# Loads of x in two halves around the first weights, the bias table as high and low parts, splits of x and of weights in turn

## The reference, cut to what matters

```python
def first_block(x, ...):
    h = rmsnorm(x, norm_mix[0])
    x = x + short_conv_mixer(h, conv_w_in[0], conv_w[0], conv_w_out[0])   # h @ w_in comes first
    ...
def differential_attention(q, k, v, lam, rel_bias):
    bucket = t5_bucket(k_pos[None, :] - q_pos[:, None])
    bias = rel_bias[bucket].astype(jnp.float32).transpose(2, 0, 1)         # 32 buckets, 4 heads
    s = jnp.einsum('bhcqd,bhcsd->bhcqs', qblk, kt).astype(jnp.float32) * scale + bias[None, :, None]
```

## Time and profile before

| | |
|---|---|
| median of three runs | 1386.07 us |
| fastest of them | 1385.76 us |
| profiled execution, its own time | 1391.24 us |
| its span, first to last instruction | 1389.4 us |
| PE busy | 1317.0 us, 95% |
| DVE busy | 1035.0 us, 74% |
| ACT busy | 855.5 us, 62% |
| first matmul of the weight stream | 19.62 us after the start of the span |

### The profile page before, as it was taken

How to read it: one execution, slowest core, us unless ns; L and a number is a source line. 1 busy time by engine, 2 the same in 40 slices (tenths; PEclk the granted TensorE clock), 3 DMA queues, 4 the chain that set the end, 5 groups by cost and what they waited for, 6 DMA issues and landing times.

```text
span 1389.4 us, 18772 instructions
## 1 busy us (share of the span) xinstructions
PE 1317.0 (95%) x6058; PEld 1073.3 (77%) x6058; DVE 1035.0 (74%) x1471; ACT 855.5 (62%) x1256; POOL 35.7 (3%) x48
## 2 busy tenths in 40 slices
PE   7999999998897999999999999999998885999998
PEld 5878888887576788888888888888876754888887
DVE  4576555567546999999999999999994846555554
ACT  4656444457344687878787878788774544544443
POOL 0000000001100000000000000000000301000000
PEclk9999999999798999999999999999999875999999
DMA  9545555554121897989898989998994400355440
GB/s 360 215 151 185 189 195 187 181 173 161 63 86 64 307 373 298 367 318 362 315 369 310 362 315 366 344 352 330 335 346 152 182 1 1 143 184 188 182 151 31
DMA packets 46121, 319.31 MB, mean 230 GB/s; under 512 B 5152, under 2 KB 6304, under 8 KB 7808
## 3 DMA queue, kind: packets, MB, share of 16 engines
q1 hardware_dynamic: 44288, 316.40, 61.0%
q10 hardware_dynamic: 1680, 2.10, 0.5%
q0 software_dynamic: 112, 0.26, 0.2%
HBM read 316.64 MB, written 2.10 MB: 229 GB/s over the span
## 4 chain that ended last, share of the span: by engine, by line
PE 85%; DVE 9%; ACT 2%; issue 2%; DMA 1%; DVEq 0%; POOL 0%; SPq 0%; ACTq 0%
PE bank L360 25%; PE bank L362 25%; PE bank L361 24%; PE bank L741 3%; DVE wl L1399 2%; PE bank L424 2%; DVE x L1906 2%; PE bank L847 1%; PE bank L396 1%; ACT wh L932 1%; DMA fixed<-fixed_dram 1%; PE bank L604 1%; PE bank L603 1%; PE bank L868 1%; DVE xtl L1419 1%
## 5 line engine op out<-in xcount | busy, mean ns | idle before, releaser
L1399 DVE TENSOR_TENSOR wl<-raw,wh 128x1024 fp32r<-128x1024 f32 x598 | 713.6, 1219 | 217.4 <-ACT wh L932 207.5
L932 ACT ACTIVATE wh<-raw 128x1024 fp32r<-128x1024 f32 x598 | 630.1, 1059 | 326.8 <-PE bank L362 319.6
L360 PE MATMUL bank<-wh,xth 128*128 128x512 f32 (+2 forms) x1170 | 467.1, 399 | 10.1 <-DVE wl L1399 4.7
L362 PE MATMUL bank<-wh,xtl 128*128 128x512 f32 (+2 forms) x1170 | 457.3, 391 | 0.0
L361 PE MATMUL bank<-wl,xth 128*128 128x512 f32 (+2 forms) x1170 | 457.0, 391 | 0.0
L360 PEld LDWEIGHTS bank<-wh,xth 128*128 128x128 f32 x1170 | 223.1, 191 | 56.4 <-issue 6.4
L362 PEld LDWEIGHTS bank<-wh,xtl 128*128 128x128 f32 x1170 | 222.6, 190 | 46.8
L361 PEld LDWEIGHTS bank<-wl,xth 128*128 128x128 f32 x1170 | 223.4, 191 | 42.5
L360 PE MATMUL bank<-wh,hth 128*128 128x512 f32 x456 | 178.5, 391 | 0.0
L362 PE MATMUL bank<-wh,htl 128*128 128x512 f32 x456 | 177.9, 390 | 0.0
L361 PE MATMUL bank<-wl,hth 128*128 128x512 f32 x456 | 177.4, 389 | 0.0
(11 more groups left out here) (288 smaller groups left out, 786.1 us busy)
## 6 DMA issues: line engine op xcount, KB each, us to landing
raw<-weights_dram SPq DMA_DIRECT2D x299, 1024.0 KB, 5.3
x<-x_dram SPq DMA_DIRECT2D x1, 1024.0 KB, 8.0
bias_scratch<-act ACTq DMA_DIRECT2D x1, 1024.0 KB, 15.8
wide<-bias_scratch ACTq DMA_DIRECT2D x8, 128.0 KB, 2.3
out_dram<-x SPq DMA_DIRECT2D x4, 256.0 KB, 2.1
fixed<-fixed_dram SPq DMA_DIRECT2D x1, 600.0 KB, 9.1
rows<-rows_dram POOLq DMA_DIRECT2D x1, 256.0 KB, 6.1
cols<-cols_dram SPq DMA_DIRECT2D x1, 73.0 KB, 8.8
```

The source lines that it names most:

```text
L360: mm(o, lh, wh[:, wi, sl], start=start, stop=False)
L362: return mm(o, ll, wh[:, wi, sl], start=False, stop=stop)
L932: A(wh[:, c % SPLIT, 0:n], raw[:, (c // 2) % RAW, (c % 2) * UNIT:(c % 2) * UNIT + n], ACT.Copy).then_inc(hi_done, 1)
L1399: V.tensor_tensor(wl[:, c % SPLIT, 0:n], raw[:, (c // 2) % RAW, (c % 2) * UNIT:(c % 2) * UNIT + n], f32(wh[:, c % SPLIT, 0:n]), ALU.subtra ...
```

## The change

- SP issues only the identity part of `fixed` early, then `cols`, the first 512 columns of x (half 0), weight panel 0, the other half of x, panel 1, the rest of `fixed`, and panels 2 to 5. Each half of x has its own semaphore.
- The spread bias table is split in a high and a low part (fp32r), and the selector is copied to fp32r. Each head is then two fp32r matmuls. Heads 0 and 1 are multiplied before the transposes of half 0, heads 2 and 3 between those of half 0 and of half 1. PE waits for the copies of heads 0 and 1 before unit 0, and for those of heads 2 and 3 before unit 4.
- ACT touches a small tile first, so that the function table is loaded there. ACT and DVE then alternate: two blocks of x, one weight unit, four times, and then units 4 and 5. DVE copies heads 2 and 3 after unit 1.
- The table goes to DRAM in four transfers, one for each head, from other tiles. ACT does not wait for them before the first layer; it waits before the read-back, and DVE waits before the first SwiGLU.
- Some semaphores are merged, with no change in the order of the work.

```diff
-            sp.dma_start(x[:, :, :], x_in.rearrange("(t p) d -> p t d", p=P)).then_inc(sem("x_in"), 16)
-            sp.dma_start(fixed[:, :], fixed_in).then_inc(sem("fixed_in"), 16)
+            sp.dma_start(fixed[:, 0:P], fixed_in[:, 0:P]).then_inc(sem("cols_in"), 16)
             sp.dma_start(cols[:, :], cols_in).then_inc(sem("cols_in"), 16)
-            for p in range(RAW):
+            halves = x_in.rearrange("(t p) d -> p t d", p=P)
+            sp.dma_start(x[:, :, 0:WIDE], halves[:, :, 0:WIDE]).then_inc(sem("x_in0"), 16)
+            sp.dma_start(raw[:, 0, :], weights[0]).then_inc(raw_full[0], 16)
+            sp.dma_start(x[:, :, WIDE:D], halves[:, :, WIDE:D]).then_inc(sem("x_in1"), 16)
+            sp.dma_start(raw[:, 1, :], weights[1]).then_inc(raw_full[1], 16)
+            sp.dma_start(fixed[:, P:NFIXED], fixed_in[:, P:NFIXED]).then_inc(sem("fixed_in"), 16)
+            for p in range(2, RAW):
                 sp.dma_start(raw[:, p, :], weights[p]).then_inc(raw_full[p], 16)
...
-            pe.wait_ge(sem("rel_in"), 32)
-            for h in range(NB2):
-                mm(bank[h][:, :], relw[:, h, :], onehot, start=True, stop=True).then_inc(sem("rel_T"), 1)
-            pe.wait_ge(sem("fixed_in"), 16)
-            for n in range(2):
-                turn_half("mix0", n, 4 + 2 * n)
-            pe.wait_ge(sem("rel_c"), NB2)
+            def rel_bias(h):
+                mm(bank[h][:, :], relh[:, h, :], picked, start=True, stop=False)
+                mm(bank[h][:, :], rell[:, h, :], picked, start=False, stop=True).then_inc(sem("rel_T"), 1)
+            rel_bias(0)
+            rel_bias(1)
+            pe.wait_ge(sem("cols_in"), 32)
+            turn_half("mix0", 0, 4)
+            rel_bias(2)
+            rel_bias(3)
+            turn_half("mix0", 1, 6)
...
             for j in range(6):
+                if j < 2:
+                    pe.wait_ge(sem("rel_c"), 2 * j + 2)
...
-            sc.wait_ge(sem("cols_in"), 16)
-            for n in range(2):
-                turned_hi("mix0", n, 4 + 2 * n)
-            for c in range(SPLIT):
+            sc.wait_ge(sem("half"), 1)
+            A(stat[:, 0:1], half[:, 0:1], ACT.Copy)
+            sc.wait_ge(sem("cols_in"), 32)
+            for c in range(4):
+                turned_hi_pair("mix0", 2 * c, 4 + c)
+                split_hi(c, 0)
+            for c in range(4, SPLIT):
                 split_hi(c, 0)
             for n in range(2):
                 squares("mix0", n)
-            sc.wait_ge(sem("rel_c"), NB2)
-            sc.dma_start(scratch[0:NB2 * P, :].rearrange("(h p) n -> p h n", p=P), act[:, 0, 0:NB2 * WIDE].rearrange("p (h n) -> p h n", h=NB2))\
-              .then_inc(sem("rel_st"), 16)
+            for h in range(NB2):
+                sc.wait_ge(sem("rel_c"), h + 1)
+                sc.dma_start(scratch[h * P:(h + 1) * P, :], rel_rows[h]).then_inc(sem("rel_st"), 16)
             sc.wait_ge(sem("ang"), 1)
             A(trig[:, :, :, :], trig[:, :, :, :], ACT.Sin).then_inc(sem("trig"), 1)
-            sc.wait_ge(sem("rel_st"), 16)
...
-            V.tensor_copy(relw[:, :, :], relb[:, :, None].to_broadcast((BUCKETS, NB2, P))).then_inc(sem("rel_w"), 1)
-            for h in range(NB2):
+            spread = relb[:, :, None].to_broadcast((BUCKETS, NB2, P))
+            mark(V.tensor_copy(picked, onehot.rearrange("p (a n) -> p a n", a=2)))
+            link(V.tensor_copy(relh, spread))
+            V.tensor_tensor(rell, spread, f32(relh), ALU.subtract).then_inc(sem("rel_w"), 1)
+            def rel_copy(h):
                 dv.wait_ge(sem("rel_T"), h + 1)
-                V.tensor_copy(act[:, 0, h * WIDE:(h + 1) * WIDE], bank[h][:, :]).then_inc(sem("rel_c"), 1)
-            dv.wait_ge(sem("cols_in"), 16)
-            turned_lo("mix0", range(0, 4), 4)
-            turned_lo("mix0", range(4, 8), 6)
-            for c in range(SPLIT):
+                V.tensor_copy(rel_rows[h], bank[h][:, :]).then_inc(sem("rel_c"), 1)
+            rel_copy(0)
+            rel_copy(1)
+            dv.wait_ge(sem("cols_in"), 32)
+            for c in range(4):
+                for k in (2 * c, 2 * c + 1):
+                    dv.wait_ge(sem("norm_hi"), 2 * c + 2)
+                    V.scalar_tensor_tensor(out=xtl[:, k, :], in0=bank[4 + c][:, (k % 2) * 256:(k % 2 + 1) * 256],
+                                           scalar=col("mix0", k), in1=f32(xth[:, k, :]), op0=ALU.mult, op1=ALU.subtract)\
+                     .then_inc(sem("norm_l"), 1)
                 split_lo(c, 0)
-
+                if c == 1:
+                    rel_copy(2)
+                    rel_copy(3)
+            for c in range(4, SPLIT):
+                split_lo(c, 0)
```

More of the change, by code:

```diff
@@ L177, in build @@
         onehot = ebuf[0:BUCKETS, 0, :]
-        relw = ebuf[0:BUCKETS, 1, :].rearrange("p (h n) -> p h n", h=NB2)
+        picked = hth[0:BUCKETS, 0:2, :]
+        relh, rell = (v[0:BUCKETS, 2:4, :].rearrange("p a (h n) -> p (a h) n", h=2) for v in (hth, htl))
+        rel_rows = (act[:, 0, 3072:3584], act[:, 1, 3072:3584], hbuf[:, 0, :], hbuf[:, 1, :])
         NORMS = ("mix0", "ffn0", "mix1", "ffn1", "attn2", "mlp2")
@@ L191, in x_ready @@
             if tag == "mix0":
-                eng.wait_ge(sem("x_in"), 16)
+                eng.wait_ge(sem(f"x_in{n}"), 16)
             elif tag == "attn2":
@@ L290, in _ @@
             g = nc.gpsimd
-            pool.dma_start(rows[:, :], rows_in.to_broadcast((P, NROWS))).then_inc(sem("rows_in"), 16)
+            pool.dma_start(rows[:, :], rows_in.to_broadcast((P, NROWS))).then_inc(sem("pos_in"), 16)
             pool.dma_start(posi[:, :], pos_in).then_inc(sem("pos_in"), 16)
@@ L314, in norm_rs @@
                 if tag in GATED:
[L315 to L318, removed]
+                    r.then_inc(sem("norm_gate"), 1)
+                    pool.wait_ge(sem("norm_gate"), 2 * GATED.index(tag) + 1)
+                    g.tensor_scalar(nrs[:, NT:2 * NT], nrs[:, 0:NT], 0.5, None, ALU.mult).then_inc(sem("norm_gate"), 1)
+                    pool.wait_ge(sem("norm_gate"), 2 * GATED.index(tag) + 2)
                     r = g.tensor_tensor(nrs[:, 2 * NT:3 * NT], nrs[:, 0:NT], nrs[:, NT:2 * NT], ALU.mult)
@@ L961, in turned_hi, with turned_hi_pair @@
                       scale=col(tag, 4 * n + k)).then_inc(sem("norm_hi"), 1)
+            def turned_hi_pair(tag, k0, b):
+                for k in (k0, k0 + 1):
+                    sc.wait_ge(sem("norm_T"), KD * nth(tag) + k0 + 2)
+                    A(xth[:, k, :], bank[b][:, (k % 2) * 256:(k % 2 + 1) * 256], ACT.Copy, scale=col(tag, k))\
+                        .then_inc(sem("norm_hi"), 1)
             def rs_ready(tag):
@@ L1300, in _ @@
                 squares("attn2", n)
+            sc.wait_ge(sem("rel_st"), 16 * NB2)
             for h in range(NB2):
@@ L1519, in _ @@
             dv.wait_ge(sem("rel_in"), 32)
-            V.tensor_copy(relw[:, :, :], relb[:, :, None].to_broadcast((BUCKETS, NB2, P))).then_inc(sem("rel_w"), 1)
-            for h in range(NB2):
-                dv.wait_ge(sem("rel_T"), h + 1)
-                V.tensor_copy(act[:, 0, h * WIDE:(h + 1) * WIDE], bank[h][:, :]).then_inc(sem("rel_c"), 1)
-            dv.wait_ge(sem("cols_in"), 16)
-            turned_lo("mix0", range(0, 4), 4)
-            turned_lo("mix0", range(4, 8), 6)
-            for c in range(SPLIT):
-                split_lo(c, 0)
-            dv.wait_ge(sem("pos_in"), 16)
+            spread = relb[:, :, None].to_broadcast((BUCKETS, NB2, P))
[3 more added lines that the diff above has]
+            def rel_copy(h):
+                dv.wait_ge(sem("rel_T"), h + 1)
+                V.tensor_copy(rel_rows[h], bank[h][:, :]).then_inc(sem("rel_c"), 1)
[8 more added lines that the diff above has]
+                     .then_inc(sem("norm_l"), 1)
+                split_lo(c, 0)
+                if c == 1:
[3 more added lines that the diff above has]
+                split_lo(c, 0)
+            dv.wait_ge(sem("pos_in"), 32)
             dv.wait_ge(sem("fixed_in"), 16)
-            dv.wait_ge(sem("rows_in"), 16)
             link(V.tensor_copy(posf[:, :], posi[:, :]))
@@ L1611, in _ @@
             dv.wait_ge(sem("norm_rs"), nth("ffn0") + 1)
+            dv.wait_ge(sem("rel_st"), 16 * NB2)
             ffn("ff", U_FF1, FF1 // FG, 2, 4, FG, 2, 0, leave=leave_ff1)
```

## The result

The changed kernel takes 1377.31 us in the median of five runs (1374.8 to 1378.57), the one before 1386.07: ratio 0.9923, 95% interval [0.9901, 0.9944]. One run of before, 2196.27 us, stands alone and does not enter the ratio. That is 8.8 us faster, where 6.2 was forecast. Its profiled execution took 1378.57 us with a span of 1376.4; the one of before had 1391.24 and 1389.4, so the two traces differ by 13.0 us, more than the medians. Where these 13.0 lie is the first question.

The account below looks back on a forecast made before the run. PE's matmul stream was taken to bound the kernel. A 4.7 us earlier start plus 1.5 us from the clock gave 6.2 us, so 1386.07 became 1379.9 us, with 1377.0 to 1382.8 called 8 in 10.

Parts of the forecast that it names:

- What bounds it: Whole kernel: PE, busy 95% of the span, bounds it, so an earlier PE start moves everything behind it.
- Step 1: Loads at the start: half 0 of x lands at 9.2 us, panel 0 at 11.7, half 1 at 12.95.
- third rival: Loads at the start: half 1 lands with panel 1 at 15.5 us; gain 3.7, 1382.4 us; chance 0.07.
- Step 2: PE before the weight stream: transposes and bias heads let it reach unit 0 at 14.9 us, 4.7 sooner.
- Step 3: Splits on ACT and DVE stay ahead of PE; unit 6 split by 30.8 us, wanted at 32.6.
- Step 4: Clock at the stream's start: full speed from 17.8 us, 2.9 at half speed, 1.5 lost instead of 2.95.
- late clock: Start of the stream: level rises 6 us after its first matmul; gain 4.7, 1381.4 us; chance 0.15.
- order: Loads at the start: half 1 shares the engines with panel 1; gain 3.7, 1382.4 us; chance 0.07.
- unit 6: Split of this weight unit comes at 34.8 us and PE stalls 2.2; 1382.1 us; chance 0.06.
- slower: Loads at the start: halves of x move at 108 GB/s, full-speed start 0.9 later; 1387.0 us; chance 0.03.
- early clock: Start of the stream: level already up, PE starts at 14.0 us; 1378.1 us; chance 0.08.

Follow-up runs that it names:

- a_again: The changed kernel, unchanged, run once more: 1375.17 us, first weight matmul at 13.3 us.
- x_whole: The changed kernel with x loaded in one transfer ahead of panel 0: first weight matmul at 16.3 us.
- bias_f32: The changed kernel with the bias table multiplied in float32, four matmuls in the new places: first weight matmul at 15.0 us.
- rows_late: The changed kernel with the load of `rows` issued only after half 1 of x has landed: first weight matmul at 13.05 us.
- loads_alone: The kernel before with only the new order and cuts of the loads: first weight matmul at 19.02 us.
- no_turns: The changed kernel without the alternation of blocks of x and weight units on ACT and DVE: first weight matmul at 17.4 us.
- warm: The changed kernel with 12 unused matmuls on PE before x is there: first weight matmul at 12.89 us.
- best: The changed kernel with unused matmuls at the start and in two later idle PE places, `rows` loaded late: 1371.78 us, 0.989 of before.

## Why the prediction was right or wrong

- **What bounds it**: right. PE was never idle from the first transpose of x to 80 us, and the shift reached the latent attention unchanged (185.0 to 185.2 us from the mark in each trace).
- **Step 1, landings**: too late, and the main reason why the start came sooner than reckoned. Half 0 landed at 8.0 (7.3 in a_again), not 9.2; half 1 at 12.0 (11.7), not 12.95. x_whole tells the terms apart. With identity and `cols` ahead of it all of x landed at 10.7, 1.05 us later than the 9.65 of before, so these two cost 1.05 us and not the 0.3 + 0.5 reckoned. The half of x that the first transposes no longer wait for brought 2.7 us (3.4 against a_again), where 420 GB/s had priced its 512 KB at 1.2. That rate was the mis-sized term; what makes those bytes slower is not shown. The distance between the halves, 3.75 forecast, was 4.0. That the order is kept was right, so the third rival fell. x_whole also shows that cutting x in two gained 2.7 to 3.3 us.
- **The cut against the rule**: the coalescing rule of the Trainium skill ("DMA: Bandwidth & Descriptors", Rules for kernel authors) pointed the other way; for these transfers, queued behind one another, this case's measurement decides against it (x and panel 0 landed by 12.0 us in three pieces, by 13.2 in two).
- **Step 2, PE up to unit 0**: the working held. 1.94, 1.99 and 1.9 us were measured for transposes, heads and transposes (1.75, 1.7 and 1.75 forecast). Since half 1 had landed when the heads ended (12.0 and 12.03), the heads cover its landing exactly, as taken. The start came 1.25 us sooner than 14.9: 0.9 from step 1's landing of half 1, 0.3 because 1.62 us passed from half 1's first transpose to the first weight matmul, where 1.95 was reckoned.
- **Step 3, ACT and DVE**: right. DVE began unit 6 at 28.0 and had it by 29.2 (30.8 forecast), with PE wanting it near 31; PE never waited for it. The store's wait was under-priced: a stall of 4 us said, 7.1 measured, 9.8 at the mark with the clock that fell behind it.
- **Step 4, the clock**: mis-sized on both sides. Full speed came 2.1 us after the first weight matmul (2.9 forecast) and 3.7 after half 1's first transpose (4.8); 1.0 us was lost, not 1.5. With PE busy up to the stream it came 1.0 us after the first weight matmul in bias_f32, 1.4 in rows_late, 2.2 in the changed kernel's two later traces, 3.5 in x_whole. With PE idle ahead of the stream it came after 6.0 and 3.3 us in the two traces of before, 4.8 in loads_alone and 4.7 in no_turns. So work ahead of the stream counts, but by how much is not settled, and the "2.95 lost before" was one draw; the other was 1.7. The rule of the Trainium skill that transposes do not count as busy in the same way ("TensorE: Matmul & The Clock Gate", Part 4) is not borne out by the 1.0 us of bias_f32, though matmuls of 32 rows ran ahead of those transposes and no run takes them away.
- **The sum and the forecast**: 6.2 us forecast, 7.5 at the mark, 8.8 between the medians. At the mark the term that failed is the earlier start: 4.7 us in the sum, 6.0 to 6.6 measured, by the landings of step 1. The clock's term, 1.5, came out at 1.3 in the mean of the traces only because both of its sides were too large. Behind the mark I carried the gain over to the median as if nothing there varied. It varies by 4.4 us between the two traces of before and by 4.5 among three of the changed kernel, and 1.3 us of the 8.8 lie there unexplained. The range 1377.0 to 1382.8 held the time by 0.3 us only, and with those 1.3 us partly by luck.
- **The chances**: here the step that failed is the premise that "about 2% (28 us) is what a measurement of this kernel can tell from no change", by which 0.98 of the chance went to a change too small to be told. No row stood behind it. The measured interval of the ratio, 0.9901 to 0.9944, is half a per cent wide and excludes no change: the kernel is faster by 0.8%, and that outcome had been given no chance of its own.
- **Rivals**: late clock, order, unit 6 and slower did not come; the early clock came in part. The angle chain had ended at 26.7 us.

## What to carry to other kernels

At a start, list all chains that end within a few us of each other (landing, first products, splits) and time each alone: the loads alone brought the first weight matmul 0.6 us forward, all parts together 6.0 to 6.6. A wait priced at nothing must be priced again after the change; the store's wait would have cost a stall of 7.1 us and 9.8 us at the mark. Work out how small a change repeated timings can tell before you call an effect too small: here four and five executions of the two kernels told 0.8% from nothing. Compare traces at a mark right behind the edit before the ends are compared, and profile the kernel before twice.

## What the runs showed of the hardware

- From 2 to 5.5 us the transfers move 108 to 175 GB/s over the twelve traces with the broadcast load, 133 and 130 in the two without it; from 8 to 12 us it is 403 to 439 in all of them.
- In warm, 3.6 us of full-array matmuls were followed by full speed from 5.75 us on, and the level fell again after 1.7 us of idleness behind transposes and matmuls of 32 rows. In best the same 3.6 us were not followed by it; the level rose at 11.2 us.
- Behind 7.19 us of float32 matmuls of 32 rows the transposes of the kernel before start 0.21 us apart, at half speed; in warm they start 0.11 apart.
- The time of stages with short PE bursts depends on the clock of the single execution: 114.3 and 117.5 us for one attention stage with the same work. Unused matmuls in one idle place of PE made it 109.2.
